# Each low product right behind its high one: pairs in place of groups of four in the weight-stationary chunks

## The reference

```python
h = einsum('bsd,de->bse', x, w_in)          # q, k, v, z_attn, u_pool, z_pool, gates
# branch A: three dilated sliding-window attentions for each of 8 head slots, merged by their denominators
y_attn = o * silu(z_attn)
# branch B: trailing mean minus token (windows 2, 4, 8, 16), a linear map per group
y_pool = causal_pool_mixer(u_pool, w_pool, pool_scale) * silu(z_pool)
merged = g_attn * (y_attn @ w_proj_attn) + g_pool * (y_pool @ w_proj_pool)
out = layer_norm(alpha * x + merged @ w_out, ln_gamma, ln_beta)
```

## Time and profile before

| what | value |
|---|---|
| median of three runs | 926.74 us (926.66 to 926.92) |
| the profiled execution's own time | 926.75 us |
| its span | 924.9 us |
| TensorE matmul (PE) busy | 917.9 us, 99% |
| TensorE weight load (PEld) busy | 784.2 us, 85% |
| VectorE busy | 720.8 us, 78% |
| ScalarE busy | 441.6 us, 48% |
| granted TensorE clock | 0.999 of full speed |
| line 526 (H), matmuls into proj_ps | 1088, 342.2 us busy |
| line 532 (L), matmuls into proj_ps | 1088, 213.9 us busy |

### The profile page before, as it was taken

One profiled execution on the slowest core, in us unless ns is written; L12 is line 12 of the kernel. 1 busy time (PEld: TensorE's weight loads), 2 busy tenths in 40 slices (PEclk: granted clock), 3 DMA queues, 4 the chain that ended last, 5 costly groups with the idle time before them and its releaser, 6 DMA issues.

```text
span 924.9 us, 11792 instructions
## 1 busy us (share of the span) xinstructions
PE 917.9 (99%) x4778; PEld 784.2 (85%) x4778; DVE 720.8 (78%) x1053; ACT 441.6 (48%) x571; POOL 0.2 (0%) x4
## 2 busy tenths in 40 slices
PE   9999999999999999999999999999999999999997
PEld 7888888888888888888888889888888888888887
DVE  6998776778876776779877778998867898766866
ACT  6555534445644435346444445545534555433340
POOL 0000000000000000000000000000000000000000
PEclk9999999999999999999999999999999999999999
DMA  9756554546454554537554554465754646668432
GB/s 375 246 182 227 181 184 143 189 165 232 162 193 158 177 195 164 182 137 247 169 190 169 182 182 161 163 249 193 281 185 140 227 175 228 227 224 323 182 137 92
DMA packets 26858, 180.79 MB, mean 195 GB/s; under 512 B 3247, under 2 KB 3503, under 8 KB 6191
## 3 DMA queue, kind: packets, MB, share of 16 engines
q1 hardware_dynamic: 25776, 173.71, 52.3%
q10 hardware_dynamic: 1028, 6.33, 1.7%
HBM read 177.93 MB, written 2.10 MB: 195 GB/s over the span
## 4 chain that ended last, share of the span: by engine, by line
PE 98%; DVE 1%; DMA 0%; ACT 0%; DVEq 0%; issue 0%
PE proj_ps L526 27%; PE proj_ps L532 14%; PE attn_ps L518 9%; PE attn_ps L520 9%; PE attn_ps L519 9%; PE proj_ps L520 4%; PE proj_ps L519 4%; PE proj_ps L518 4%; PE mixed_ps L520 2%; PE mixed_ps L518 2%; PE mixed_ps L519 2%; PE value_ps L520 2%; PE value_ps L518 2%; PE value_ps L519 2%; PE mixed_ps L642 1%; PE proj_ps L567 1%
## 5 line engine op out<-in xcount | busy, mean ns | idle before, releaser
L1252 DVE TENSOR_TENSOR w_lo<-w_raw,w_hi 128x1024 fp32r<-128x1024 f32 (+1 forms) x354 | 405.4, 1189 | 60.5 <-ACT w_hi L911 60.0
L911 ACT ACTIVATE w_hi<-w_raw 128x1024 fp32r<-128x1024 f32 (+1 forms) x354 | 347.9, 1029 | 214.3 <-PE attn_ps L520 72.9
L526 PE MATMUL proj_ps<-xt,w_hi 128*128 128x512 f32 x1088 | 342.2, 396 | 0.0
L532 PEld LDWEIGHTS proj_ps<-xt,w_lo 128*128 128x128 f32 x1088 | 204.4, 188 | 48.2
L532 PE MATMUL proj_ps<-xt,w_lo 128*128 128x256 f32 x1088 | 213.9, 278 | 0.0
L526 PEld LDWEIGHTS proj_ps<-xt,w_hi 128*128 128x128 f32 x1088 | 165.9, 189 | 0.5
L918 ACT ACTIVATE corr<-proj_ps 128x256 f32<-128x256 f32 x70 | 26.8, 383 | 197.8 <-PE proj_ps L532 194.8
L518 PE MATMUL attn_ps<-w_hi,xt 128*128 128x512 f32 x235 | 91.4, 389 | 0.0
L519 PE MATMUL attn_ps<-w_lo,xt 128*128 128x512 f32 x235 | 91.4, 389 | 0.0
L520 PE MATMUL attn_ps<-w_hi,xt 128*128 128x512 f32 x235 | 91.4, 389 | 0.0
L1116 DVE TENSOR_TENSOR qk_f<-proj_ps,corr 128x256 f32<-128x256 f32 x46 | 19.5, 423 | 68.4 <-ACT corr L918 68.3
(11 more groups left out here) (287 smaller groups left out, 1226.0 us busy)
## 6 DMA issues: line engine op xcount, KB each, us to landing
w_raw<-in_weights SPq DMA_DIRECT2D x158, 1024.0 KB, 4.8
first_raw<-in_first SPq DMA_DIRECT2D x8, 640.0 KB, 7.8
bias_rows<-in_gate_bias ACTq DMA_DIRECT2D x4, 512.0 KB, 3.9
res<-in_x_rows ACTq DMA_DIRECT2D x1, 2048.0 KB
out_rows<-res SPq DMA_DIRECT2D x8, 256.0 KB, 2.1
gamma<-in_gamma_row ACTq DMA_DIRECT2D x1, 1024.0 KB
beta<-in_beta_row ACTq DMA_DIRECT2D x1, 1024.0 KB
mask<-in_mask SPq DMA_DIRECT2D x1, 512.0 KB, 18.0
```

What stands on the lines that cost most here:

```text
L526: mm(bank, w_hi[:, slot, k * P:(k + 1) * P], tile.rearrange("p a s -> p (a s)"), start=first, stop=False)
L532: done = mm(bank[:, SEQ:2 * SEQ], w_lo[:, slot, k * P:(k + 1) * P], tile[:, 0, :], start=False, stop=last)
L911: activation(w_hi[:, i % RING, cols], w_raw[:, n % RING, cols], ACT.Copy).then_inc(hi_split, 1)
L1252: tt(w_lo[:, i % RING, cols], w_raw[:, n % RING, cols], w_hi[:, i % RING, cols].bitcast(F32), ALU.subtract).then_inc(lo_split, 1)
```

## The change

One constant, the default of `together` in `chunk`, goes from 2 to 1:

```diff
 LINE = 512
-TOGETHER = 2
+TOGETHER = 1
 COMBOS_AT = 3
```

## The result

The changed kernel takes 929.16 us (median of 14 runs, 927.86 to 931.0), the kernel before 926.86 us in runs beside it (14, 926.65 to 927.64). The ratio is 1.0022, with a 95% interval from 1.0014 to 1.0031: 2.3 us more, a slight slowdown, clear of zero and a little above the 0.2% (1.85 us) up to which the prediction speaks of no change. The forecast was 928.2, in a range of 925.2 to 930.9.

A forecast was written before the change was run, and what follows sets the result against it. TensorE's own pace was taken to bound the kernel. From 926.75 us, +1.0 for the order and +0.44 for the early wait gave 928.2 us, in a range of 925.2 to 930.9.

The forecast's parts named there:

- What bounds the kernel: In the changed stretch only TensorE's own pace sets the time; each added nanosecond per matmul is paid in full.
- The wait: At the first chunk, the first H waits for VectorE's low part: +0.44 us, paid to the end; no second wait.
- Term 1: The new order's cost over 1104 pairs in 69 chunks, taken as +1.0 us.
- The distances as they stand: Adding measured H to L and L to H starts gives 349.3 ns a pair against 348.4, +0.9 ns.
- the give-back to 346.6: Rival for the chunks' pairs: they give back mixing's cost and fall to 346.6 ns, 925.2 us; chance 0.07.
- worse than that: Rival for the chunks' pairs: each size change disturbs the pace, 353.5 ns or more, 932.8 us and above; chance 0.10.
- The likeliest case: Forecast for the chunks and first wait: +1.0 and +0.44 us, own range 927.4 to 929 us; chance 0.35.
- The uniform pace: Lower bound from same-size matmuls elsewhere: 346.6 ns for one of each, saving 1.8 ns a pair, −2.0 us.
- the group behind the scores: Far upper bound from a group following the scores: 353.5 ns a pair, +5.1 ns, or +5.6 us.
- The load: Weight loads under L in the chunks: 0.114 to 0.120 us just covers 0.11; no load gets less cover, though tight.
- The trace has no steady H L H L: No steady alternation with these sizes in the earlier trace, so the order's cost was bounded by other rows.

The follow-up runs named there:

- the run of the wait alone: Against the kernel before, order H H L L kept, each half waits once, for the low part, ahead of its first H: 927.66 us against 926.99, ratio 1.0007.
- groups of four: Against the kernel before, TOGETHER = 4 (H H H H L L L L), waits as before: 929.05 us, ratio 1.0023.
- 384 columns: Order H L H L, with the low product streaming 384 columns in place of 256: 995.65 us, ratio 1.0740 to the kernel before.
- the kernels with a fixed start in every chunk or half chunk: H L H L with H H L L for the first two tiles of each chunk or half chunk, waits as before: 929.59 us (1.0028) and 927.99 (1.0012).
- a start of one or two other groups, put by the profile: H L H L with one or two H H L L groups at places chosen for the fast pattern, waits as before: 925.53 us, ratio 0.9985.
- the eight-group kernel: Against the kernel before, TOGETHER = 8, eight H then eight L, a half chunk each, waits as before: 927.51 us, ratio 1.0005.

## Why the prediction came out as it did

**What bounds the kernel**: right in the main. TensorE's pace sets the time, but "a nanosecond more for each matmul there is paid in full" is not quite so: in three heads TensorE had waited for VectorE ahead of the transposes, and 0.39 us of the slower pace went into that slack. The earlier trace rows lists waits of matmuls, and these stood on loads.

**The wait**: right, 0.41 us against 0.44 in the changed kernel and 0.40 in the run of the wait alone. No second wait came.

**The order**: the direction was right, the size was not: 2.3 us in the profile instead of 1.0. This is the step that failed, Term 1, and the way of it was wrong too. "The distances as they stand" took each distance between two starts for a property of the two matmuls, so that they could be put together in another order. They are not: groups of four should have been faster by that sum and were slower by 2.1 us. A distance hangs on the state that the matmuls ahead have left, and each order has repeating patterns of its own. H L H L has two, and what I had as rivals, the give-back to 346.6 and the "worse than that" of 353.5, turned out to be both of them, in one execution. The likeliest case, one pace of 349.3, did not occur in any stretch of H L H L. That the time came out near the forecast and inside the range is in part luck. It is a mean of the two patterns, about two thirds slow and one third fast. All slow, it would be 926.75 + 1104 × 5.0 / 1000 + 0.44 = 932.7 us, above the 930.9 of the range, and the prediction gave that side 0.10. The uniform pace is the fast pattern to 0.1 ns and the group behind the scores the slow one to as little, but it is not shown that they are the same states: with 384 columns the fast pattern lies 6.8 ns above the uniform pace. The size by counts is (705 × 5.0 − 399 × 1.7) / 1000 = 2.8 us if the 669 and 378 are scaled to 1104 pairs, and that is what the chunks became longer by; the stretch says 2.3, since 0.39 us went into the waits at the transposes and the rest, 0.12, came back in small parts at other joints.

**The load**: that no load loses cover was right, and "tight" was the wrong worry. With a longer low product the excess grew.

**"The trace has no steady H L H L"** I read as a lack of data. That the groups of before alternate, 233 236 116 112 and then 232 231 114 119, stood in the trace, and was averaged away in the prediction; it was the sign that the pace has a memory longer than one group.

**The spread of the changed kernel's runs** was not foreseen at all. That the entry into a pattern is decided anew in each execution would explain it, and the kernels with a fixed start in every chunk or half chunk spread over less than 1 us. But no two profiles of one kernel show it; it stays argued.

## What to carry to other kernels

Where TensorE is the bound and matmuls of two sizes alternate, measure the pace over several groups and look at the single starts: an order can lock into patterns that differ by 2%, and what stands ahead of it chooses. Don't add up pairwise distances to forecast another order; bound it with the pace of uniform matmuls below and the worst group seen above. And a start of one or two other groups, put by the profile, can be worth more than the order itself (925.5 against 929.2 us here, 0.4 of it from the wait), though it has to be checked again whenever the code ahead of it changes.

## What the runs showed of the hardware

At one size matmuls stand 227 ns apart with 512 columns and 120 with 256, and 227 whether the weights or the activations are the stationary operand. Mixed, 512 and 256 in turn settle at 346.7 or 353.4 ns a pair, 512 and 384 at 406.7 or 413.3; the two levels are 7 ns apart in both. Groups of two, four and eight settle at 348.4, 350.8 and 349.2, the last from the eight-group kernel's timeline of PE:

```profile
107.73 2.00 PE L526 MATMUL proj_ps<-xt,w_hi 128*128 128x512 f32 x8
...
116.11 2.00 PE L526 MATMUL proj_ps<-xt,w_hi 128*128 128x512 f32 x8
```

where 24 pairs take 8.38 us. The slow pattern repeats after three pairs, and it shifts against the tiles k, so it does not go with the tile's address. What holds this state is open. Too short a cover for the load is ruled out by the 384 columns, where every load has about 173 ns or more over it against the 0.11 us that one needs. Against VectorE's and ScalarE's work as the cause speaks only that a pattern runs unchanged through chunks in which their work comes and goes; no run tried it, and nothing here looks further inside.
